# All eight token tiles per weight step, and a first stage on x without its norm, in a two-layer streaming encoder block

## What is computed

```python
h = rms_norm(x, norm_g)                    # x / sqrt(mean(x*x) + eps) * g
proj = h @ w_in
(q, k, v, z_a, p_in, z_b, u, v_sgu, z_c, glu_a, glu_b, z_d, merge) = split(proj)
q = apply_rope(rms_norm(q, q_norm_g), cos, sin)
k = apply_rope(rms_norm(k, k_norm_g), cos, sin)
o_a = window_attention(q, k, v, attn_sinks)
o_b = multiscale_pool(p_in, pool_mix, pool_scale)
o_c = spatial_gating(u, v_sgu, ...)        # u * (position mix of layer_norm(v_sgu))
o_d = conformer_conv(glu_a, glu_b, ...)
mixed = sum over branches of sigmoid(merge) * ((o * silu(z)) @ w_branch)
return x + mixed @ w_out
```

## Time and profile before

| | us |
|---|---|
| median of 3 runs (2106.82 to 2107.40) | 2107.12 |
| the profiled execution | 2107.21 |
| its span, first to last instruction | 2105.4 |
| TensorE busy | 2081.7 |
| VectorE busy | 1284.6 |
| GpSimd busy | 1291.1 |
| ScalarE busy | 823.1 |
| mean granted TensorE clock, share of full | 0.997 |

### The profile page before, as it was taken

How to read it: one execution, slowest core, us unless ns; L and a number is a source line. 1 busy time by engine, 2 the same in 40 slices (tenths; PEclk the granted TensorE clock), 3 DMA queues, 4 the chain that set the end, 5 groups by cost and what they waited for, 6 DMA issues and landing times.

```text
span 2105.4 us, 27266 instructions
## 1 busy us (share of the span) xinstructions
PE 2081.7 (99%) x9772; PEld 1720.3 (82%) x9772; DVE 1284.6 (61%) x1502; ACT 823.1 (39%) x1579; POOL 1291.1 (61%) x987
## 2 busy tenths in 40 slices
PE   6999999999999999999999999999999999999999
PEld 5898877788888888888888887778888888888887
DVE  6875544588878745335378845447888786452331
ACT  5433644334233435324444245443432333443331
POOL 5457544676669767654455665447766696675543
PEclk9999999999999999999999999999999999999999
DMA  5322232312441334414543132323234213434153
GB/s 187 87 68 96 66 116 85 118 53 66 85 96 43 79 77 85 139 55 147 159 129 98 56 104 87 100 86 101 61 80 89 69 51 82 89 71 140 50 200 100
DMA packets 114565, 197.25 MB, mean 94 GB/s; under 512 B 12288, under 2 KB 21760, under 8 KB 114432
## 3 DMA queue, kind: packets, MB, share of 16 engines
q1 hardware_dynamic: 97728, 165.29, 25.7%
q0 software_dynamic: 9216, 16.78, 5.9%
q10 hardware_dynamic: 7488, 13.44, 1.7%
HBM read 153.52 MB, written 41.94 MB: 93 GB/s over the span
## 4 chain that ended last, share of the span: by engine, by line
PE 94%; POOL 2%; DVE 1%; ACT 1%; issue 1%; DMA 0%; DVEq 0%; SPq 0%; POOLq 0%; ACTq 0%
PE acc L639 79%; PE acc L687 6%; PE aux L687 4%; POOL wlo L564 1%; PE aux L759 1%; PE aux L778 1%; PE aux L769 1%; POOL wsum L568 1%; PE aux L722 1%; PE aux L793 1%; PE aux L735 0%; PE aux L800 0%; PE acc L832 0%; DVE pool L1309 0%; ACT prob L1108 0%
## 5 line engine op out<-in xcount | busy, mean ns | idle before, releaser
L564 POOL TENSOR_TENSOR wlo<-raw,whi 128x512 fp32r<-128x512 f32 x464 | 634.2, 1368 | 545.3 <-ACT whi L900 544.6
L639 PE MATMUL acc<-fhi,whi 128*128 128x512 f32 x2048 | 801.7, 391 | 1.9 <-DVE blo L1312 1.9
L639 PE MATMUL acc<-fhi,wlo 128*128 128x512 f32 x2048 | 797.2, 389 | 0.0
L639 PE MATMUL acc<-flo,whi 128*128 128x512 f32 x2048 | 797.0, 389 | 0.0
L900 ACT ACTIVATE whi<-raw 128x512 fp32r<-128x512 f32 x464 | 290.7, 627 | 516.8 <-PE acc L639 383.8
L639 PEld LDWEIGHTS acc<-fhi,whi 128*128 128x128 f32 x2048 | 384.4, 188 | 83.8 <-issue 3.7
L639 PEld LDWEIGHTS acc<-fhi,wlo 128*128 128x128 f32 x2048 | 384.4, 188 | 80.7
L639 PEld LDWEIGHTS acc<-flo,whi 128*128 128x128 f32 x2048 | 384.6, 188 | 78.4 <-issue 0.2
L564 POOL TENSOR_TENSOR wlo<-wsum,whi 128x512 fp32r<-128x512 f32 x192 | 271.1, 1412 | 171.4 <-ACT whi L900 171.0
L1316 DVE SCALAR_TENSOR_TENSOR aux<-conv,allp,aux 128x1024 f32<-128x1024 f32 x232 | 299.1, 1289 | 20.0 <-issue 0.4
L639 PE MATMUL acc<-bhi,whi 128*128 128x512 f32 x512 | 201.8, 394 | 0.0
(11 more groups left out here) (183 smaller groups left out, 2352.3 us busy)
## 6 DMA issues: line engine op xcount, KB each, us to landing
raw<-wstream SPq DMA_DIRECT2D x464, 256.0 KB, 2.7
md<-prev POOLq DMA_DIRECT2D x64, 256.0 KB, 4.2
x<-x SPq DMA_DIRECT2D x32, 256.0 KB, 4.8
md<-prev SPq DMA_DIRECT2D x32, 256.0 KB, 3.6
out<-x ACTq DMA_DIRECT2D x32, 256.0 KB, 2.3
mx<-md SPq DMA_DIRECT2D x24, 256.0 KB, 4.8
qd<-qst ACTq DMA_DIRECT2D x16, 256.0 KB, 2.3
qs<-qd SPq DMA_DIRECT2D x16, 256.0 KB, 2.7
```

The source lines that it names most:

```text
L564: nc.gpsimd.tensor_tensor(wlo[:, f % SLOTS, :], src, whi[:, f % SLOTS, :].bitcast(F32), ALU.subtract).then_inc(lo_made, 1)
L639: mm = nc.tensor.matmul(dst, w, m[:, kt0 + k, cols], start=first and k == 0 and n == 0, stop=last and k == UK - 1 and n == 2, skip_group_c ...
```

## The change

- PLAIN has three entries: VS, Q, KV. A step takes one unit against all eight token tiles (24 matmuls), tiles 4 to 7 first (VS and Q in `aux`, tiles 0 to 3 in `acc`; KV in `aux` alone). Each of the 20 units of a layer is loaded and split once.
- VS runs on g\*x instead of h (`x_rounded`, `x_rest`), in slots of its own (`X_SLOT`); the norm is put back per token afterwards, in the statistics of the layer norm and in `normal_vs` on ScalarE. In layer 1, g\*x is made during the last stage of layer 0.
- The norms of layer 0 come from a second copy of x, token-major (`x_rows`, eight loads of 512 KB), squared and summed by ScalarE (`row_squared`). In layer 1 `token_sums` stands inside the first VS step. `rms_diagonals`, `spread` and GpSimd's adds of squares are gone. The reciprocals (128 x 8) are written to HBM (`store_norms`) and read back on all partitions (`load_spread`, 512 KB). From there VectorE makes h for both halves (`h_all`), during VS.
- GpSimd makes the forms of h (`form`, eight operations of 128 x 1024), after its work for Q6, Q7, KV0 and KV1. x22 has its sign turned, so `sum_x` subtracts.
- q is first copied out of PSUM (`take_q`), and all of its squaring, normalising and rotating comes after Q. `sgu_mix` stands after KV step 2 and before p7 of the first pair of U, with `row_sums` after KV step 0.
- On VectorE, the last two `form_rest` and two of the four `mix_taken` move into stage U; q chunks 2 and 3 are rotated in the steps of U, and both chunks of k after it. `turn_q` 3 waits for all six rotations.
- The warm-up has 22 matmuls in place of 16 and waits for no data.

The diff, cut to its core (of blocks that are replaced as a whole, the removed lines are left out):

```diff
-WARMUP = 16
+WARMUP = 22
...
-PLAIN = (("VS0", 8), ("VS1", 8), ("Q1", 8), ("KV1", 4), ("Q0", 8), ("KV0", 4))
+PLAIN = (("VS", 8), ("Q", 8), ("KV", 4))
...
+        X_SLOT = {(0, 0): S_B11, (0, 1): S_F6, (1, 0): S_F5, (1, 1): S_B21}
...
+        FORM_AT = {("Q", 6): (0, 1), ("Q", 7): (2, 3), ("KV", 0): (4, 5), ("KV", 1): (6, 7)}
...
+            def load_x(k):
+                for t in range(2):
+                    sp.dma_start(x_block(k, t), x[k * P:(k + 1) * P, t * HALF:(t + 1) * HALF]).then_inc(x_loaded[k], 16)
+                    if (k, t) == (0, 0):
+                        sp.dma_start(allp[:], cols).then_inc(cols_loaded, 16)
+                load_unit(0, "VS", k)
+
+            def load_row(t):
+
+                if t >= 4:
+                    sp.wait_ge(rows_squared, t - 3)
+                sp.dma_start(xrow[:, t % 4, :], x_rows[t * P:(t + 1) * P, :]).then_inc(row_loaded[t % 4], 16)
+
+            for k, tiles in enumerate(((), (0,), (1, 2), (3, 4), (5, 6), (7,), (), ())):
+                load_x(k)
+                for t in tiles:
+                    load_row(t)
+            sp.dma_start(ident[:], ident_in).then_inc(ident_loaded, 16)
...
+            def form(L, n):
+
+
+                at = slice(n % 2 * 2, n % 2 * 2 + 2)
+                b11, b12, b22, b21 = (q[:, at, :] for q in (x11, x12, x22, x21))
+                if n == 0:
+                    pool.wait_ge(h_ready, (L + 1) * 2 * KT)
+                if n >= 4:
+                    pool.wait_ge(form_made, 8 * L + n - 1)
+                if n < 2:
+                    op = nc.gpsimd.tensor_tensor(b11, b11, b12, ALU.subtract)
+                elif n < 4:
+                    op = nc.gpsimd.tensor_tensor(b12, b22, b12, ALU.subtract)
+                elif n < 6:
+                    op = nc.gpsimd.tensor_tensor(b22, b22, b11, ALU.add)
+                else:
+                    op = nc.gpsimd.tensor_tensor(b21, b22, b21, ALU.subtract)
+                op.then_inc(form_made, 1)
...
-                        if (L, name, k) == (0, "VS0", SLOTS):
-                            for e in range(1, KT):
-                                pool.wait_ge(xsq_ready, KT + e + 1)
-                                if e > 1:
-                                    pool.wait_ge(xsq_pooled, e - 1)
-                                add(sumsq[:, HALF:SEQ], sumsq[:, HALF:SEQ], sqs[:, e, :], xsq_pooled)
                         low(L, loaded(L, name, k), name, k)
+                        for n in FORM_AT.get((name, k), ()):
+                            form(L, n)
...
+                    if name == "VS":
+                        pe.wait_ge(x_ready, x_turn(L, k, 1) + 1)
+                    if name == "Q":
+                        pe.wait_ge(h_ready, (L * KT + k + 1) * 2)
+                    for n_tile, tile in enumerate((4, 5, 6, 7, 0, 1, 2, 3)):
+                        if name == "VS" and L and k == 0:
+                            if n_tile >= 4:
+                                pe.wait_ge(taken["abcd"[tile]], L * BANK_N["abcd"[tile]])
+                            if n_tile == 6:
+                                token_sums(L)
+                            if n_tile == 7:
+                                pe.wait_ge(rms_root, L + 1)
+                        if name == "Q" and k == 0 and n_tile % 2 == 0:
+                            pe.wait_ge(vs_taken, 8 * L + 2 * (n_tile // 2 + 1))
+                        if name == "KV" and k == 0:
+                            pe.wait_ge(q_taken, 4 * L + 2)
+                        if name == "KV":
+                            dst = aux[:, tile // 4, tile % 4 * width:(tile % 4 + 1) * width]
+                        else:
+                            dst = tile_bank(tile)
...
             def turn_q(L, n):
 
                 tiles = ((4, 5), (6, 7), (0, 1), (2, 3))[n]
-                pe.wait_ge(kv_taken, 4 * L + 4)
-                pe.wait_ge(roped, 6 * L + (1, 2, 4, 5)[n])
+                pe.wait_ge(sgu_taken, 4 * L + 4)
+
+                pe.wait_ge(roped, 6 * L + (1, 2, 3, 6)[n])
                 if n >= 2:
...
+                token_major(L, "VS", 8)
+                token_major(L, "Q", 8)
+                token_major(L, "KV", 4, {0: lambda L=L: row_sums(L), 2: lambda L=L: sgu_mix(L, (0, 1))})
+                pe.wait_ge(sgu_taken, 4 * L + 2)
+                pair(L, "U", 0, {"p7": lambda L=L: sgu_mix(L, (2, 3))})
+                pair(L, "U", 1, {"p2": lambda L=L: (pe.wait_ge(ident_loaded, 16), turn_q(L, 0)),
+                                  "p4": lambda L=L: turn_q(L, 1)})
...
+            def store_norms(L):
+                act.wait_ge(norms_made, L + 1)
+                act.dma_start(rd[L].rearrange("t p -> p t"), rms[:], allow_slow_non_contiguous=True).then_inc(norms_stored, 16)
+            def load_spread(L):
+                act.wait_ge(norms_stored, 16 * (L + 1))
+                act.dma_start(spreads[:], rd[L:L + 1].rearrange("o t p -> o (t p)").partition_broadcast(P)
+                              ).then_inc(spread_loaded, 16)
+            def x_rounded(L, k, t):
+                nc.scalar.activation(fhi[X_SLOT[k // UK, t]][:, k % UK, :], x_block(k, t), ACT.Copy,
+                                     scale=allp[:, L, C_G + k:C_G + k + 1]).then_inc(x_hi, 1)
+            def h_rounded(L, k):
+                act.wait_ge(step_done, stepped(L, "VS", k))
+                for t in range(2):
+                    act.wait_ge(h_scaled, (L * KT + k) * 2 + t + 1)
+                    copy(fhi[H_SLOT[k // UK, t]][:, k % UK, :], x_block(k, t)).then_inc(h_hi, 1)
...
+                    load_spread(L)
+                    next_high(L, "VS", 4)
+                    for k in range(5):
+                        h_rounded(L, k)
+                next_high(L, "VS", 5)
+                h_rounded(L, 5)
+                next_high(L, "VS", 6)
+                h_rounded(L, 6)
+                act.wait_ge(half_done, 2 * L + 1)
+                take_vs(L, 4)
+                take_vs(L, 6)
+                act.wait_ge(step_done, stepped(L, "VS", 7))
+                take_vs(L, 0)
+                take_vs(L, 2)
+                h_rounded(L, 7)
+                next_high(L, "VS", 7)
+                next_high(L, "Q", 0)
+                next_high(L, "Q", 1)
+                act.wait_ge(sgu_var, L + 1)
+                nc.scalar.activation(rstd[:, 0, :], mv[:, :, 1], ACT.Sqrt, bias=epst[:]).then_inc(sgu_root, 1)
+                next_high(L, "Q", 2)
+                normal_vs(L, range(3))
+                next_high(L, "Q", 3)
+                form_rounded(L, 0)
+                form_rounded(L, 1)
+                normal_vs(L, range(3, 6))
+                next_high(L, "Q", 4)
+                form_rounded(L, 2)
+                form_rounded(L, 3)
+                normal_vs(L, range(6, TT))
+                next_high(L, "Q", 5)
+                form_rounded(L, 4)
+                form_rounded(L, 5)
+                next_high(L, "Q", 6)
+                act.wait_ge(half_done, 2 * L + 2)
+                take_q(L, 0)
+                take_q(L, 1)
                 square_q(L, 0)
+                next_high(L, "Q", 7)
+                take_q(L, 2)
+                take_q(L, 3)
                 square_q(L, 1)
                 root(L, 0, 16)
+                square_q(L, 2)
                 root(L, 1, 16)
+                square_q(L, 3)
+                root(L, 2, 16)
+                root(L, 3, 16)
+                for k in range(4):
+                    next_high(L, "KV", k)
...
+            def x_rest(L, k, t):
+                dve.wait_ge(x_hi, x_turn(L, k, t) + 1)
+                s = X_SLOT[k // UK, t]
+                scaled(flo[s][:, k % UK, :], x_block(k, t), allp[:, L, C_G + k:C_G + k + 1],
+                       fhi[s][:, k % UK, :].bitcast(F32), ALU.subtract).then_inc(x_ready, 1)
+
+            def h_scale(L, k, t):
+                scaled(x_block(k, t), x_block(k, t), allp[:, L, C_G + k:C_G + k + 1],
+                       spreads[:, t * HALF:(t + 1) * HALF], ALU.mult).then_inc(h_scaled, 1)
...
                 mean_squares(L, 0)
                 mean_squares(L, 1)
                 normalise(L, 0)
+                row_bias()
+                mean_squares(L, 2)
                 normalise(L, 1)
+                mean_squares(L, 3)
                 rotate(L, 0)
                 normalise(L, 2)
+                normalise(L, 3)
                 mix_taken(L, 0)
                 mix_taken(L, 1)
                 rotate(L, 1)
                 mean_squares(L, 4)
+                mean_squares(L, 5)
                 normalise(L, 4)
                 normalise(L, 5)
+
+                def last_forms():
+                    form_rest(L, 6)
+                    form_rest(L, 7)
+
+                def last_mixes():
+                    dve.drain()
+                    mix_taken(L, 2)
+                    mix_taken(L, 3)
 
                 for i in range(2):
                     a_, b_ = oc[:, 2 * i, :], oc[:, 2 * i + 1, :]
+                    turns = rotate_steps(L, 2 + i)
```

(17 more changed lines are left out.)

466 lines of the change are left out of this document (199 added, 267 removed).

## The result

The changed kernel takes 2114.7 us (median of 6 runs, 2112.22 to 2116.0) against 2107.26 of the kernel before in the same series: ratio 1.0036, 95% interval 1.0025 to 1.0047. It is slower by 0.4%, where faster was forecast. The time lies inside the range, between the rival with the slow store (C, 2110) and the one in which VectorE is the bound (B, 2119). The profiled execution is the fastest of the six: 2112.22, span 2110.2, TensorE busy for 2079.6.

The account below looks back on a forecast made before the run. TensorE, busy for 2081.7 of 2105.4 us, was taken as the bound. 2107.1 less 16.7 (layer 0's start) less 1.9 (layer 1) plus 12.4 (new waits after Q) gave 2101 us, range 2087 to 2119.

Parts of the forecast that it names:

- C: Rival, chance 0.14: the norms' store is slow, near 13 us, and delays Q in layer 0; +9, 2110 us.
- B: Rival, chance 0.27: VectorE, taking turns with GpSimd, is the bound between Q and ZC; 15.3 a layer, 2119 us.
- TensorE's work: Stage lengths on TensorE: VS and Q 43.5 us each, KV's first matmul to U's 27.5.
- The start of VS: Layer 0: VS starts at 8.4 us; up to 5.6 us later would cost nothing.
- I take 4.0: Layer 0, before Q: the store of the norms to HBM takes 4.0 us, between 2.3 and 6.6.
- My upper bound, 6.6: Most the norms' store could take: 2.3 us plus 56 more packets per engine at 76 ns each.
- The slow clock behind that wait: Layer 0, start of Q: after a 5.6 us wait TensorE runs at half clock, costing 1.7 us.
- Who is late next: VectorE beside GpSimd after Q: waits of 1.1 and 3.4 us plus 1.7 of half clock, 6.2 a layer.
- K+48.4: Stage U, K being KV's first matmul: `sum_22` ends there, p4 wants its bank at K+47.4, 1.1 us waited.
- T+9.7: T being the end of U: k's last rotation ends there; `turn_q` 3, wanted at T+6.3, waits 3.4 us.
- my layout: Operation lists laid out by hand after Q, with about half of VectorE's operations in turns with GpSimd: 6.2 us a layer.
- A: Rival, chance 0.15: no new waits after Q, as GpSimd's operations fall between VectorE's; 2088.5 us.

Follow-up runs that it names:

- The probes: The kernel before with five, then nine small stores one by one behind its end: 1024 adjacent elements took 10.5 and 8.8 us, 128 pieces of 32 bytes 1.4.
- turn4: The change, but `turn_q` 3 waits for the four rotations of q alone and the first load of q for all six: 2103.97 us.
- mix_first: The change, but in stage U VectorE does the second part of q's rotation after `sum_22`, not before: 2120.48 us.
- small_low: The change, with GpSimd's operations for U and ZC cut to 64 of 512 columns: 2096.7 us.
- rows_store: The change, but layer 0's tokens are reordered so the norms are stored as 128 pieces of 32 bytes, not 1024 single elements: 2107.34 us.
- between: The change, but q's third chunk is rotated between the two pairs of U, not inside the first: 2107.09 us.
- all_five: The change with vs copies early, rope tables before `h_all`, norms stored in 32-byte pieces, `turn_q` 3 waiting for q alone, between, forms one unit earlier: 2082.24 us.
- four_slow: all_five with the change's store of 1024 single elements and the old token order put back: 2083.99 us.
- early_rope: The change, with ScalarE's copies of vs after `h_rounded` 1 in layer 0 and rope tables made before `h_all` in both layers: 2104.99 us.

## Why the prediction was wrong

**TensorE's work: right. The start of VS: 1.7 late, at no price.** The stages have the lengths of the forecast: Q, from its first matmul to KV's, 43.5 us plus the slow start (45.97 in all), from KV to U 27.44 (27.5). VS began at 10.08, not 8.4, which cost nothing, as said, since the norms set the start of Q. Layer 1's first stage has no wait, as said.

**The step that failed: "I take 4.0, nearer the lower row, since a 4-byte packet moves next to nothing".** The store took 10.66 in layer 0 and 9.4 in layer 1. My upper bound, 6.6, was also too low. Both ends came from rows on long packets (stores of 256 KB, packets of 1.8 KB), and I let a count of packets times a price per packet decide, in a regime of which no row told anything. The probes show that the price is real with nothing else running (8.8 and 10.5), and that neither the count nor the bytes make it: the pieces are neighbours, and their writes land late; spread out, my 2.3 to 6.6 would have held (3.2). That rival C, with its store near 13, had 0.14 was too little weight for a term without a like in the rows. The rest of the chain was near: load back 3.78 (3.4), `h_all` up to the 14th `h_scale` 18.0 (17), a rounding and two copies 1.7 (1.8). Together Q started at 65.70 and not at 57.5: 8.2 late, 6.7 of it by the store.

**The slow clock behind that wait: 2.4 and not 1.7.** The first 12 matmuls took 5.13 and the next 2.75 in place of 2.72 each. The length of the wait doesn't give the length of the spell: after 14.6 us in turn4 the first 12 took 4.36, after 14.5 in mix_first 5.41.

**Who is late next: right in place, too small in size.** `sum_22` was to end at K+48.4 and ended at K+49.4 (161.02, K being 111.67), so p4 waited 2.1 and not 1.1. The last rotation of k was to end at T+9.7 and ended at T+9.8; `turn_q` 3 waited 3.57 (3.4). The spells of half clock were taken too small: I had one a layer, 1.7, and there are two. In layer 0 the 60 matmuls behind p4 take 15.45 where they take 13.6 at full clock (96 in 21.81 in between), and the transposes and 24 matmuls behind `turn_q` 3 take 8.16 where they take 6.33: 3.65 in all. In layer 1 it is 0.3 and 1.8 (13.90 and 8.10). So the two waits cost 9.3 us in layer 0 and 7.7 in layer 1, against 6.2 each, 17.0 in all against 12.4. The table shows less of it for layer 0, since 1.7 us that I hadn't counted went from the same stretch; 1.1 of them is a wait in the attention that only the kernel before has:

```profile
PE aux L769 <- DVE prob L1306: 1.1, 1, 1.1
```

Why this wait is gone was not tried. small_low shows the mechanism to be the one named, and turn4 that k's rotations in front of `turn_q` 3 were it.

**The rivals.** C is what happened in the first place: its sign, a store of norms over 6 us, came. Its 2110 against 2112.2 in the profiled execution is partly luck: it took a store near 13, and with 10.66 its rule gives 2108. That rule, that each us beyond 4.0 delays Q by as much, held nearly in rows_store: the store 5.6 shorter, Q 4.9 earlier. B (turns of VectorE) added at most 3.1 and 1.5 in the two layers beyond my layout, not 9.1 each. A did not happen as the kernel stood, but turn4 and between show that both waits were a matter of order.

**Why the median is above the profiled execution.** The start differs from execution to execution: with the same first stage, the store took 10.66 in the change's profile, 12.19 in turn4's and 11.08 in between's, and the wait before Q 11.8, 14.6 and 13.2. all_five, where the store is short and little waits for it, has a spread of 1.2 us in four runs, the change 3.8 in six. But rows_store, with the short store, has 3.5 in ten, so the store isn't the whole cause; what the rest is stays open.

**What I overlooked.** I took for granted that the norms' trip sets the start of Q. It did so only because ScalarE's copies of vs stood behind `h_rounded` 6. With the copies earlier, the tables made while VectorE idles, and the forms earlier, the slow store costs under 2 us (four_slow). The idea with these orders is worth 23 us against before (all_five); as it was written it is about 31 us short of that.

## What to carry to other kernels

A transfer whose shape has no like in the trace is not bounded by the nearest rows: measure it by itself at the end of the program, and beside traffic too, since the store in pieces of 32 bytes took 1.4 us there and 5.08 in its place. When work gets a long new chain, look first at what stands behind it in the queues of the engines and doesn't need it: moving the copies and the tables ahead was worth 9.7 us (early_rope), shortening the chain 7.4 (rows_store), and with all orders mended the shorter chain was worth under 2. Moving the copies alone gave 5.1, for the chain ended in the next wait. Where VectorE is late beside GpSimd, move its two-operand work into its own idle time, not just one step back, since the operation behind it may free a bank.

## What the runs showed of the hardware

- 1024 single 4-byte elements stored to adjacent places of HBM take 8.8 to 10.5 us with nothing else running, 128 of them 7.4 to 8.6; 1024 at a distance of 512 bytes 3.2; 128 pieces of 32 bytes 1.4.
- Read the other way it isn't slow: the load of 1024 adjacent single elements in rows_store (`rms<-rd`) took 4.2 us beside other traffic, where the store of 128 pieces of 32 bytes took 5.08.
- In these slow stores the DMA engines are done early: the packets of the 1024 adjacent elements are through 1.7 us after the issue, and the store lands 7 us after that.
- A store of 128 adjacent pieces of 32 bytes takes 1.4 us alone and 5.08 beside the weight loads.
- Waits of 2.1 and 3.6 us in stages that are otherwise full are followed by a lower granted clock (0.75 and 0.66 over 5 us); what that costs differs, 0.3 and 1.8 us behind the same 2.1 us wait in the two layers. Taking away 3.57 us twice (turn4) gained 10.7; taking away 4.5 us in all (between: 2.1 twice at p4 and 0.6 twice at `turn_q` 3, with 0.4 twice new) gained 7.6.
